# GpSimd makes the last Newton steps, and TensorE and ScalarE the last two tiles' sums, at the end of a fused encoder layer

## The reference, cut to what matters

```python
# x: (1, 1024, 1024) float32; h: the stream after the mixing sub-layer
u = rms_norm(h, g_pre_mlp[l])
f = jnp.square(jax.nn.relu(jnp.einsum('bsd,df->bsf', u, w_ff_in[l])))
y = jnp.einsum('bsf,fd->bsd', f, w_ff_out[l])
h = h + rms_norm(y, g_post_mlp[l])

def rms_norm(x, g):
    y = x * lax.rsqrt(jnp.mean(x * x, axis=-1, keepdims=True) + EPS)
    return y * g
```

## Time and profile before

| | |
|---|---|
| median of 3 runs | 1052.81 us (1050.79 to 1053.06) |
| the profiled execution | 1052.49 us, of which 1050.8 us are the span from first to last instruction |
| TensorE busy | 1009.5 us (96%) |
| VectorE busy | 801.1 us (76%) |
| ScalarE busy | 568.5 us (54%) |
| GpSimd busy | 92.4 us (9%) |
| granted TensorE clock, mean | 0.988 |
| last matmul starts | 1030.89 us |
| first and last store of the output issued | 1037.05 and 1047.76 us |

### The profile page before, as it was taken

One profiled execution on the slowest core, in us unless ns is written; L12 is line 12 of the kernel. 1 busy time (PEld: TensorE's weight loads), 2 busy tenths in 40 slices (PEclk: granted clock), 3 DMA queues, 4 the chain that ended last, 5 costly groups with the idle time before them and its releaser, 6 DMA issues.

```text
span 1050.8 us, 12384 instructions
## 1 busy us (share of the span) xinstructions
PE 1009.5 (96%) x4940; PEld 816.1 (78%) x4940; DVE 801.1 (76%) x752; ACT 568.5 (54%) x747; POOL 92.4 (9%) x71
## 2 busy tenths in 40 slices
PE   7999999998999999999999999999999999999992
PEld 5878777886767787788788888788888788888782
DVE  6247659698577579977878867998777998768998
ACT  7423532658758536677653557343666434565453
POOL 0013213121312143000000000000000000000000
PEclk9999999999989999999999999999999999999997
DMA  9421111200001544013013022031031031043003
GB/s 327 140 71 41 41 41 41 80 1 2 23 20 41 203 155 164 1 41 120 1 49 112 1 89 72 1 101 60 1 120 41 1 120 41 1 163 158 1 0 160
DMA packets 38656, 74.64 MB, mean 71 GB/s; under 512 B 3236, under 2 KB 12744, under 8 KB 38600
## 3 DMA queue, kind: packets, MB, share of 16 engines
q1 hardware_dynamic: 38600, 73.86, 20.3%
HBM read 65.46 MB, written 8.39 MB: 70 GB/s over the span
## 4 chain that ended last, share of the span: by engine, by line
PE 89%; DVE 6%; ACT 2%; issue 2%; DMA 0%; SPq 0%; ACTq 0%; DVEq 0%
PE ps L700 27%; PE ps L702 27%; PE ps L704 27%; PE ps L911 2%; PE ps L865 2%; PE ps L936 1%; PE ps L769 1%; DVE out_gained L2038 1%; DVE y L1991 1%; DVE a_op L1937 1%; DVE y L2097 1%; ACT sb_w L1291 1%; PE ps L800 1%; ACT sb_r L1287 0%; DVE b_op L1948 0%
## 5 line engine op out<-in xcount | busy, mean ns | idle before, releaser
L700 PE MATMUL ps<-a_op,b_op 128*128 128x512 f32 x448 | 175.5, 392 | 4.0 <-issue 1.3
L700 PE MATMUL ps<-b_op,a_op 128*128 128x512 f32 x448 | 174.7, 390 | 3.6 <-issue 3.6
L704 PE MATMUL ps<-a_op,b_op 128*128 128x512 f32 x448 | 174.4, 389 | 0.0
L702 PE MATMUL ps<-a_op,b_op 128*128 128x512 f32 x448 | 174.3, 389 | 0.0
L704 PE MATMUL ps<-b_op,a_op 128*128 128x512 f32 x448 | 174.3, 389 | 0.0
L702 PE MATMUL ps<-b_op,a_op 128*128 128x512 f32 x448 | 174.3, 389 | 0.0
L700 PE MATMUL ps<-act_hi,w_hi 128*128 128x512 f32 x288 | 115.4, 401 | 7.2 <-DVE act_lo L1633 7.2
L1445 ACT CAST a_op<-f 128x1024 fp32r<-128x1024 f32 x56 | 58.8, 1050 | 112.9 <-PE ps L704 72.8
L1948 DVE TENSOR_TENSOR b_op<-wq,b_op 128x1024 fp32r<-128x1024 f32 x96 | 117.1, 1219 | 0.0
L702 PE MATMUL ps<-act_lo,w_hi 128*128 128x512 f32 x288 | 113.0, 392 | 0.0
L704 PE MATMUL ps<-act_hi,w_lo 128*128 128x512 f32 x288 | 112.8, 392 | 0.0
(11 more groups left out here) (216 smaller groups left out, 1672.2 us busy)
## 6 DMA issues: line engine op xcount, KB each, us to landing
wq<-in_w_ff_in SPq DMA_DIRECT2D x16, 1024.0 KB, 5.3
wq<-in_w_ff_out SPq DMA_DIRECT2D x16, 1024.0 KB, 5.1
stage<-in_w_in SPq DMA_DIRECT2D x16, 512.0 KB, 4.6
y<-in_x SPq DMA_DIRECT2D x4, 1024.0 KB, 12.5
stage<-in_w_out SPq DMA_DIRECT2D x8, 512.0 KB, 4.2
h_spill<-y SPq DMA_DIRECT2D x8, 512.0 KB, 2.7
h_back<-h_spill SPq DMA_DIRECT2D x2, 2048.0 KB, 11.7
out<-y SPq DMA_DIRECT2D x8, 512.0 KB, 2.7
```

What stands on the lines that cost most here:

```text
L700: nc.tensor.matmul(dst, stat[0], mov[0], start=first, stop=False, skip_group_check=chained)
L702: nc.tensor.matmul(dst, stat[0], mov[1], start=False, stop=False, skip_group_check=chained)
L704: return nc.tensor.matmul(dst, stat[1], mov[0], start=False, stop=last, skip_group_check=chained)
```

## The change

- *VectorE* no longer makes `var` and the Newton steps of the end, nor the final tiles 6 and 7. The gains are made on whole rows of 1024 columns (`gained`), in the order of tiles 0, 1, 2, 3, 6, 7, 4, 5, and the eight half rows that stood ahead of `var_b` stand behind it.
- *GpSimd* makes the variance and the Newton steps of all four sets, in six instructions a set, each but a set's last followed by a wait for itself.
- *ScalarE* writes for tiles 6 and 7 a 128x128 matrix with `rstd` on its diagonal (`rstd_diag`), and copies the two tiles' sums out of PSUM.
- *TensorE* makes `h_back + rstd * out_gained` for tiles 6 and 7 in banks 0 to 3: identity times `h_back`, and then the diagonal matrix times `out_gained`, both in plain float32.
- *SyncE* issues the stores in the order of tiles 0, 1, 6, 2, 3, 7, 4, 5.

```diff
+        FINAL_SETS = ((0, 1, 2, 3), (4, 5), (6,), (7,))
+        BY_TENSOR = {6: 0, 7: 2}
+        GAINED = (0, 1, 2, 3, 6, 7, 4, 5)
+
+        def final_count(i):
+            return 1 + [i in tiles for tiles in FINAL_SETS].index(True)
...
         (SyncE)
-            for i in range(TOK):
-                sp.wait_ge(out_ready, i + 1)
+            for i in (0, 1, 6, 2, 3, 7, 4, 5):
+                if i in BY_TENSOR:
+                    sp.wait_ge(out_by_act, i - 5)
+                else:
+                    sp.wait_ge(out_ready, i + 1)
                 sp.dma_start(out[0, P * i:P * (i + 1), :], y[:, i, :]).then_inc(out_stored, 16)
...
         (GpSimd)
+            pool.wait_ge(var_b_ready, 1)
+            for tiles in FINAL_SETS:
+                cols = slice(tiles[0], tiles[-1] + 1)
+                v, r0, t = var[:, cols], rs0[:, cols], rs_t[:, cols]
+                pool.wait_ge(sumsq_ready, 4 * TOK + tiles[-1] + 1)
+                after(nc.gpsimd.tensor_scalar(t, sumsq[:, cols], 1.0 / D, None, ALU.mult))
+                after(nc.gpsimd.tensor_tensor(v, t, var_b[:, cols], ALU.add))
+                pool.wait_ge(rs0_ready, N_ROOTS + 1 + tiles[-1])
+                after(nc.gpsimd.tensor_tensor(t, r0, r0, ALU.mult))
+                after(nc.gpsimd.tensor_tensor(t, t, v, ALU.mult))
+                after(nc.gpsimd.tensor_scalar(t, t, -0.5, 1.5, ALU.mult, ALU.add))
+                nc.gpsimd.tensor_tensor(rstd[:, cols], t, r0, ALU.mult).then_inc(final_rstd, 1)
...
         (TensorE)
+            pe.wait_ge(h_loaded, 32)
+            pe.wait_ge(dve_evicted, dve_reads(N_PRODUCTS - 1))
+            for i, bank in BY_TENSOR.items():
+                for c in range(2):
+                    nc.tensor.matmul(ps[:, bank + c, :], ident[:, :],
+                                     h_back[1][:, i - 4, BANK * c:BANK * (c + 1)],
+                                     start=True, stop=False)
+            for i, bank in BY_TENSOR.items():
+                pe.wait_ge(diag_ready, i - 5)
+                pe.wait_ge(out_gain_done, GAINED.index(i) + 1)
+                for c in range(2):
+                    mm = nc.tensor.matmul(ps[:, bank + c, :], rstd_diag[:, i - 6, :],
+                                          out_gained[1][:, i - 4, BANK * c:BANK * (c + 1)],
+                                          start=False, stop=True)
+                mm.then_inc(sums_in_banks, 1)
...
         (ScalarE)
+            for i in BY_TENSOR:
+                act.wait_ge(final_rstd, final_count(i))
+                nc.scalar.activation(rstd_diag[:, i - 6, :], ident[:, :], ACT.Copy,
+                                     scale=rstd[:, i:i + 1]).then_inc(diag_ready, 1)
+            for i, bank in BY_TENSOR.items():
+                act.wait_ge(sums_in_banks, i - 5)
+                nc.scalar.copy(y[:, i, :], ps[:, bank:bank + 2, :].rearrange("p b n -> p (b n)"))\
+                    .then_inc(out_by_act, 1)
...
         (VectorE)
-                if n == N_PRODUCTS - 2:
-                    dve.wait_ge(rows_loaded, 32)
-                    dve.wait_ge(b_lo_ready, halves(STAGES - 1, P4))
-                    for i in range(4):
-                        gained_half(i, 0)
...
             last_tile_sum(0)
-            for i in range(4):
-                gained_half(i, 1)
-            for t in range(1, 4):
-                last_tile_sum(t)
+            gained(0)
+            gained(1)
+            last_tile_sum(1)
+            gained(2)
+            gained(3)
+            last_tile_sum(2)
+            dve.wait_ge(dve_evicted, last_sum[2])
+            gained(6)
+            last_tile_sum(3)
+            dve.wait_ge(dve_evicted, last_sum[3])
+            for i in (7, 4, 5):
+                gained(i)
             dve.wait_ge(h_loaded, 32)
-            dve.wait_ge(var_b_ready, 1)
-            final_rsqrt(range(4), 1)
-            dve.wait_ge(out_gain_done, 16)
-            for i in range(4):
-                final_tile(i)
-            final_rsqrt((4, 5), 2)
-            final_tile(4)
-            final_tile(5)
-            for i in (6, 7):
-                final_rsqrt((i,), i - 3)
+            for i in range(6):
+                dve.wait_ge(out_gain_done, GAINED.index(i) + 1)
+                dve.wait_ge(final_rstd, final_count(i))
                 final_tile(i)
```

More of the change, by code:

```diff
@@ L158, in encoder_layer @@
                     at("y_gained2", [P, 2, D], ACT_AT + 24 * K))
+        rstd_diag = at("rstd_diag", [P, 2, P], X_AT + 32 * K)
         out_gained = (at("out_gained0", [P, 4, D], X_AT), at("out_gained1", [P, 4, D], ACT_AT + 32 * K))
@@ L261, in encoder_layer @@
         var_b_ready, eps_row_ready = sem("var_b_ready"), sem("eps_row_ready")
+        final_rstd, diag_ready, sums_in_banks, out_by_act = (
+            sem("final_rstd"), sem("diag_ready"), sem("sums_in_banks"), sem("out_by_act"))
         h_loaded, out_gain_done, out_ready, out_stored = (
@@ L675, in keep_before @@
                     .then_inc(beta_masked, 1)
-            for n in range(HEADS):
-                if n == 2 * SUM_UNIT - 2:
+            for head in range(HEADS):
+                if head == 2 * SUM_UNIT - 2:
                     sum_squares(1, [win_sq[:, 0, :], win_sq[:, 1, :]])
-                keep_before(n)
+                keep_before(head)
             sum_squares(2, [work[:, 4, :], work[:, 5, :]])
@@ L2033, in evict, with gained @@
                     evict_hidden(n, s, i)
-            def gained_half(i, c):
-                cols = slice(BANK * c, BANK * (c + 1))
-                nc.vector.tensor_tensor(out_gained[i // 4][:, i % 4, cols], y[:, i, cols], rs_row[:, cols],
+            def gained(i):
+                nc.vector.tensor_tensor(out_gained[i // 4][:, i % 4, :], y[:, i, :], rs_row[:, :],
                                         ALU.mult).then_inc(out_gain_done, 1)
@@ L2100, in final_tile @@
                                                op0=ALU.mult, op1=ALU.add).then_inc(out_ready, 1)
[L2102 to L2110, removed]
-                dve.wait_ge(rstd_ready, N_ROOTS + count)
+            last_sum = {}
             def last_tile_sum(t):
@@ L2120, in last_tile_sum @@
                     .then_inc(dve_evicted, 1)
-                dve.wait_ge(dve_evicted, n_evicted[0])
-                gained_half(4 + t, 0)
+                last_sum[t] = n_evicted[0]
+            dve.wait_ge(rows_loaded, 32)
+            dve.wait_ge(b_lo_ready, halves(STAGES - 1, P4))
             dve.wait_ge(dve_evicted, n_evicted[0])
-            for i in range(4, TOK):
-                gained_half(i, 1)
             dve.wait_ge(sumsq_ready, 4 * TOK)
@@ L2132, in _ @@
             last_tile_sum(0)
-            for i in range(4):
-                gained_half(i, 1)
-            for t in range(1, 4):
-                last_tile_sum(t)
-            dve.wait_ge(h_loaded, 32)
-            dve.wait_ge(var_b_ready, 1)
-            final_rsqrt(range(4), 1)
-            dve.wait_ge(out_gain_done, 16)
-            for i in range(4):
-                final_tile(i)
-            final_rsqrt((4, 5), 2)
-            final_tile(4)
-            final_tile(5)
-            for i in (6, 7):
-                final_rsqrt((i,), i - 3)
+            gained(0)
[10 more added lines that the diff above has]
+                gained(i)
+            dve.wait_ge(h_loaded, 32)
+            for i in range(6):
+                dve.wait_ge(out_gain_done, GAINED.index(i) + 1)
+                dve.wait_ge(final_rstd, final_count(i))
                 final_tile(i)
```

## The result

The changed kernel took 1056.43 us (median of 10 runs, 1052.76 to 1057.63), the kernel before on the same chip 1051.14 (10 runs, 1049.10 to 1053.31). The ratio is 1.0038, with a 95% interval of 1.0025 to 1.0050: slower by 0.4%, some 4 us (it is taken over all the runs; the two medians alone lie 5.3 us apart). The forecast was 1057.2, in a range of 1052.4 to 1060.9. The profiled execution took 1057.63 us with a span of 1055.9.

The account below looks back on a forecast made before the run. VectorE was taken to set the end, stores close beneath. GpSimd's blocked steps put tile 6's store at 1046.0; 1046.0 + 2.6 + 5 x 1.30 + 0.4 = 1055.5, 4.7 us more; 1052.49 + 4.7 = 1057.2, range 1052.4 to 1060.9.

Parts of the forecast that it names:

- the exclusion: VectorE instructions with two SBUF inputs and GpSimd instructions reading SBUF exclude each other; the second waits for the whole first.
- VectorE's end: VectorE's last final tile, with six instead of eight to make, was to end at 1043.5 including the slowdown by GpSimd.
- root of tile 6: Tile 6's finished rstd, after six GpSimd steps at one per gap between VectorE instructions, expected at 1039.7 to 1041.0.
- root of tile 7: Tile 7's finished rstd from GpSimd, expected after VectorE's last instruction, with three or four steps undisturbed: 1044.4.
- 0.09 us to VectorE per gap: Each of VectorE's last nine two-input instructions was to grow by 0.09 us as GpSimd slips in between.
- The diagonal: ScalarE's writing of the 128-column matrix with rstd on its diagonal, taken as 0.3 us.
- A GpSimd step: One undisturbed tiny dependent instruction of GpSimd's sets, taken as 0.24 us, bounded by 0.18 to 0.37.
- The matmuls at half clock: TensorE's two diagonal matmuls for a tile, taken as 3.4 us instead of 1.7 after TensorE's idling.
- No exclusion: Rival: GpSimd's tiny steps aren't blocked beside VectorE, transfers bound; 1050.6 in all, 1.9 us faster; chance 0.16.
- No gap: Rival: GpSimd gets in at no gap of an unbroken VectorE run; 1060.8 in all; chance 0.11.
- two per gap: Rival: two GpSimd instructions get in per gap between VectorE's; 1052.7 in all; chance 0.13.
- point of decision: For slower: tile 7's root at 1039.7; each microsecond behind it is one at the end.

Follow-up runs that it names:

- e1: Changed kernel with the Newton steps back on VectorE in two sets, GpSimd idle at the end; ratio 0.9999 to the kernel before.
- e2: Changed kernel with VectorE's last nine whole-row instructions taking their second input from PSUM, results not the layer's; ratio 0.9991 to the kernel before.
- e3: Changed kernel with the stores issued in the order of tiles 0 to 7; ratio 1.0012 to the kernel before.
- e5: Changed kernel with tiles 6 and 7 in one GpSimd set, six steps instead of twelve; ratio 1.0046 to the kernel before.
- e8: Changed kernel with stores in tile order and four extra float32 matmuls ahead of each of TensorE's two diagonal waits; ratio 1.0017 to the kernel before.
- e6: Kernel before with only the variance and Newton steps of all four sets moved to GpSimd; ratio 0.9990 to the kernel before.
- e4: Changed kernel with ScalarE copying tile 6 out before it waits for tile 7's root; ratio 1.0045 to the kernel before.
- e9: Changed kernel with stores in tile order and extra float32 matmuls, four ahead of tile 6's diagonal wait, two ahead of tile 7's; ratio 0.9992.

## Why the prediction was right, and where its sizes were off

The mechanism is the one forecast: GpSimd's tiny dependent steps get in once per VectorE instruction, ScalarE's diagonals wait for them, and SyncE waits for ScalarE. e1 takes the steps off GpSimd and e2 takes the exclusion away; either removes the loss. e3 shows that the store order carries most of it on to the end. Step by step, in microseconds from the last product matmul:

| step | predicted | measured |
|---|---|---|
| first store | 5.9 | 5.9 |
| VectorE's end | 12.6 | 11.8 |
| root of tile 6 | 8.8 to 10.1 | 7.1 |
| root of tile 7 | 13.5 | 12.4 |
| diagonal of tile 7 done | 13.9 | 12.9 |
| store of tile 6 | 15.1 | 13.8 |
| from it to the end | 9.5 | 9.6 |
| end | 24.6 | 23.4 |

The time alone is a weak test. It was laid on an execution of 1052.49 us; laid on the median of ten runs of the kernel before, 1051.14, the same 4.7 us give 1055.8, about as near to the measured 1056.43 as 1057.2 is. The growth is 5.3 us by the medians, 4.0 by the ratio and 3.5 in the tail. The tail is the sharpest of the three, and there the growth was forecast a third too large, by the terms below.

**The term that was mis-sized: 0.09 us to VectorE per gap.** It came from one scan of 2.11 instead of 2.02, laid on nine instructions. Measured is next to nothing: 3.50 for three and 7.26 for six with GpSimd slipping in, 3.48 and 7.23 in e2 without it, which is 0.05 us for all nine. That is the 0.8 us in VectorE's end, and since tile 7's root follows that end, two thirds of the 1.2 us by which the tail is shorter than forecast. Another 0.3 is in the last steps: three of tile 7's were expected after VectorE's end at the soonest, and only two were left. From the diagonal to the store of tile 6 it is 0.9 us instead of 1.2, and from there to the end 0.1 more than forecast.

**Tile 6's root** came 1.7 earlier than the range had it. Its first step went through free, 0.06 us ahead of the first gain (1033.59 against 1033.65), since the set of tiles 4 and 5 had ended at 1033.62, 1.1 into the tail instead of 1.3 to 2.5. Tile 6's early root by itself changed nothing, because ScalarE wanted tile 7's diagonal before it copied tile 6; but the free step is why only two steps, not three, were left behind VectorE's end.

**The diagonal** took 0.40, not 0.3; the copy of tile 6 started 0.1 before it ended (1045.26 against 1045.36) and took that back. **A GpSimd step** undisturbed stands 0.27 behind the last, within the bounds of 0.18 to 0.37 but above the 0.24 taken. **The matmuls at half clock** took 3.78 rather than 3.4, hidden as said, if narrowly: in the changed kernel tile 7's copy ends at 1050.24 and its store goes out at once, at 1050.27, while the transfers of the three stores before it still run (share 1.01 from 1050 to 1051, 0.92 in the next microsecond). They are not hidden in e3 and e5.

**The rivals.** *No exclusion* is e2's case; it would have ended at 18.0, as its sum had it (1048.9 - 1030.89). *No gap* and *two per gap* fall by the count of nine steps beside nine instructions. The forecast's *point of decision*, tile 7's root 8.8 into the tail, is borne out by e1 (root at 4.8, no loss) and the changed kernel (12.4, 3.5 us of loss for 3.6 us of lateness).

**Three of my later expectations failed** on what lies around this. e8 is told above. e6 was priced with VectorE's end 2.0 us later than it came; its waits for GpSimd were 0.36 and 1.18 us, less than the small steps that it no longer makes. e5 halved the steps, but all six were blocked, and TensorE was idle long enough to meet them at 1.2 GHz. Besides, e1's tail is 1.8 us above its expectation without a known cause, and e4's 0.5.

**Open.** The steps of the first two sets fall in two patterns. In the changed kernel, e2, e3, e4 and e9 the set of tiles 4 and 5 ends 1.1 to 1.2 into the tail; in e5 and e8 it ends at 2.4 (e5: 1032.64 + 1.05 - 1031.26), and tile 6's root 2.4 us later than otherwise. The first step that differs is the first set's second: it begins 0.03 us ahead of a gain in the changed kernel (1028.21 against 1028.24) and takes 0.20 us, and 0.02 ahead of it in e5 (1026.98 against 1027.00), where it takes 1.30. So a hundredth of a microsecond may decide it. I don't know what tips it from one execution to the next.

## What to carry to other kernels

Small dependent steps are cheap on GpSimd (0.27 us each) only while VectorE is not in a run of instructions with two SBUF inputs; beside one, a chain moves one step per VectorE instruction (1.04 to 1.26 us, for steps of one column as of four). Before moving a chain to another engine, count its steps against the instructions it will run beside, and find who waits for its last result: blocked steps cost some 4 us here, and nothing that the times show in e6. A store queue issued in a fixed order turns the latest tile into everyone's delay: put what may be late at its end. And work given to an idle TensorE costs what the granted clock makes of it, here 3.78 us instead of 1.98 for four records, so the gain of a shortened chain can go there.

## What the runs showed that I had not expected

- VectorE pays next to nothing when a blocked GpSimd instruction gets in between two of its own: 1.21 us per final tile with it (7.26 for six), 1.20 without (7.23).
- A wait of 1.63 us on TensorE left the clock at 1.00 (e9), one of 6.15 us did not (e5). Waits shown as 3.75 us led to 2.60 us for tile 6's matmuls in the changed kernel, 2.86 in e3 and 3.78 in e4: the same wait can meet either level, or a change between them.
- The stretch up to the last product matmul, nearly the same instructions in all kernels, varied by 4.8 us between profiles (1027.67 to 1032.50), more than the change is worth. It goes with the granted clock around 305 us, far ahead of any edit, as these windows show, of e9 first and of the changed kernel below:

```profile
305.00:310.00 5.00, 3.72 (x23) 2.50 (x23) 4.97 (x3) 4.78 (x8) 1.49 (x2) 1.00 0.00 2
```

```profile
305.00:310.00 5.00, 4.37 (x13) 1.92 (x13) 4.94 (x4) 1.86 (x4) 0.15 (x2) 0.50 0.01 2
```

  e9 has 1.00 all through and the earliest last matmul. e1 to e4 have 0.69 to 0.84 in this window, 1.00 in the next, and start the last product matmul at 1028.30 to 1029.04; the kernel before, the changed one and e5 to e8 have 0.50 here, 0.57 to 0.80 in the next, and start it at 1030.53 to 1032.50. The ten runs of the changed kernel fall in the same way: 1052.76 and 1053.22 us at a mean clock of 0.996, 1054.42 and 1054.67 at 0.990, and the other six, 1056.38 to 1057.63, at 0.988. What tips the clock there is not shown. Single spans would have misled; times counted from a common event leave this out.
